# First stage of a two-block transformer kernel: separate columns for two weight chunks, earlier weight transfers, squares on GpSimd

## What is computed

```python
h = rmsnorm(x, a_norm1[i])                      # x: 1 x 512 x 1024
z = h @ a_w_in[i]                               # 1024 x (2 * 768 + 256)
u  = jax.nn.gelu(z[..., :TOK_WIDTH])            # TOK_WIDTH = 768
vv = jax.nn.gelu(z[..., TOK_WIDTH:2 * TOK_WIDTH])
q_mem = z[..., 2 * TOK_WIDTH:]
tok = gmlp_spatial_gating(u, vv, ...)
mem_o = memory_attention(q_mem, mem, a_mem_norm[i], a_w_mem_kv[i])
```

## Time and profile before

| what | value |
|---|---|
| median of 3 runs | 1449.86 us (1449.11 to 1451.22) |
| the profiled execution, its own time | 1451.27 us |
| its span, first to last instruction | 1449.5 us |
| TensorE matmuls, busy | 1438.8 us (99% of the span) |
| VectorE / ScalarE / GpSimd, busy | 961.8 / 669.5 / 41.0 us |
| granted TensorE clock, mean | 1.000 |

### The profile page before, as it was taken

One profiled execution on the slowest core, in us unless ns is written; L12 is line 12 of the kernel. 1 busy time (PEld: TensorE's weight loads), 2 busy tenths in 40 slices (PEclk: granted clock), 3 DMA queues, 4 the chain that ended last, 5 costly groups with the idle time before them and its releaser, 6 DMA issues.

```text
span 1449.5 us, 20006 instructions
## 1 busy us (share of the span) xinstructions
PE 1438.8 (99%) x7041; PEld 1151.6 (79%) x7041; DVE 961.8 (66%) x1579; ACT 669.5 (46%) x1100; POOL 41.0 (3%) x82
## 2 busy tenths in 40 slices
PE   8999999999999999999999999999999999999999
PEld 7978888888888887777778888888888877777777
DVE  5656777777766647555556777777677666666774
ACT  7445444444442235445454444444323356665662
POOL 0000000000001110000000000000111000000000
PEclk9999999999999999999999999999999999999999
DMA  6323222332346733212132322323677511112122
GB/s 227 124 96 117 73 90 98 101 97 91 101 138 236 235 112 119 76 59 88 61 100 73 101 90 98 101 90 115 203 241 234 163 56 59 59 58 74 59 82 94
DMA packets 44445, 162.66 MB, mean 112 GB/s; under 512 B 5076, under 2 KB 5844, under 8 KB 44384
## 3 DMA queue, kind: packets, MB, share of 16 engines
q1 hardware_dynamic: 33984, 126.44, 26.5%
q0 software_dynamic: 9104, 33.06, 6.7%
q10 hardware_dynamic: 1296, 2.36, 0.4%
HBM read 159.72 MB, written 2.12 MB: 112 GB/s over the span
## 4 chain that ended last, share of the span: by engine, by line
PE 93%; DVE 4%; DMA 2%; ACT 1%; issue 1%; POOL 0%; ACTq 0%; DVEq 0%; POOLq 0%
PE ps L383 17%; PE ps L384 17%; PE ps L385 17%; PE ps L399 5%; PE ps L401 5%; PE ps L400 5%; PE ps L1872 3%; PE ps L1874 3%; PE ps L1873 3%; PE ps L486 3%; PE ps L563 2%; PE ps L2050 1%; PE ps L551 1%; PE ps L1806 1%; PE ps L1808 1%; DVE wl L309 1%
## 5 line engine op out<-in xcount | busy, mean ns | idle before, releaser
L309 DVE TENSOR_TENSOR wl<-raw,wh 128x1024 fp32r<-128x1024 f32 (+3 forms) x199 | 253.9, 1276 | 119.0 <-ACT wh L303 118.8
L303 ACT CAST wh<-raw 128x1024 fp32r<-128x1024 f32 (+3 forms) x199 | 217.7, 1094 | 228.1 <-PE ps L385 194.8
L383 PE MATMUL ps<-xh,wh 128*128 128x512 f32 x720 | 281.1, 390 | 0.6 <-DVE hb L1416 0.6
L385 PE MATMUL ps<-xh,wl 128*128 128x512 f32 x720 | 280.2, 389 | 0.0
L384 PE MATMUL ps<-xl,wh 128*128 128x512 f32 x720 | 280.1, 389 | 0.0
L383 PEld LDWEIGHTS ps<-xh,wh 128*128 128x128 f32 x720 | 135.1, 188 | 30.0 <-issue 2.0
L384 PEld LDWEIGHTS ps<-xl,wh 128*128 128x128 f32 x720 | 135.1, 188 | 28.3 <-issue 0.5
L385 PEld LDWEIGHTS ps<-xh,wl 128*128 128x128 f32 x720 | 135.1, 188 | 28.2
L399 PE MATMUL ps<-xh,wh 128*128 128x512 f32 x344 | 144.5, 420 | 0.7 <-DVE wl L309 0.7
L383 PE MATMUL ps<-hth,wh 128*128 128x512 f32 x352 | 136.9, 389 | 0.0
L384 PE MATMUL ps<-htl,wh 128*128 128x512 f32 x352 | 136.9, 389 | 0.0
(11 more groups left out here) (310 smaller groups left out, 2337.3 us busy)
## 6 DMA issues: line engine op xcount, KB each, us to landing
raw<-w_a_f SPq DMA_DIRECT2D x44, 512.0 KB, 3.2
raw<-w_b_f SPq DMA_DIRECT2D x44, 512.0 KB, 3.2
row<-w_c_rows POOLq DMA_DIRECT2D x32, 512.0 KB, 4.6
row<-w_ada_rows POOLq DMA_DIRECT2D x24, 512.0 KB, 4.7
raw<-w_a_f SPq DMA_DIRECT2D x16, 704.0 KB, 4.1
raw<-w_b_f SPq DMA_DIRECT2D x16, 704.0 KB, 4.2
raw<-w_b_pair SPq DMA_DIRECT2D x18, 512.0 KB, 3.3
raw<-w_front SPq DMA_DIRECT2D x16, 512.0 KB, 3.3
```

Of the source, the lines that this page charges most:

```text
L303: nc.scalar.copy(wh[:, s, :width], raw[:, s, :width]).then_inc(w_hi, 1)
L309: nc.vector.tensor_tensor(wl[:, s, :width], raw[:, s, :width], wh[:, s, :width].bitcast(F32), ALU.subtract).then_inc(w_lo, 1)
L383: nc.tensor.matmul(dst, a, h(k), start=(k == 0), stop=False)
L385: mm = nc.tensor.matmul(dst, b, h(k), start=False, stop=(k == total - 1))
```

## The change

- Chunks 2 and 3 get columns of their own (`FRONT_COL`: from column 512 and from column 640 of their halves), beside chunks 0 and 1, which lie in the first 384 columns. So their loads no longer wait for the low parts of chunks 0 and 1, but only for the landing of chunks 0 and 1 (`w_raw` at 16), and their casts no longer wait for matmuls.
- SyncE's order: chunk 2 now ahead of x2 (rows 2, 3), the wait for x0 gone, chunk 3 ahead of x3, chunk 4 ahead of x4 (before, behind it), chunk 5 ahead of the two memory tiles.
- ScalarE squares only the row pairs 4, 5 and 6, 7. GpSimd squares the pairs 0, 1 and 2, 3 and adds the two.
- ScalarE and VectorE treat chunk 2 ahead of the rows 2 and 3.
- VectorE's first addition is gone and the second stands ahead of the low part of row 7.
- `mid()` stands inside block 7 of the first group, behind its first two token blocks (six matmuls); in the second group it stands where it was.

```diff
+FRONT_COL = {2: 512, 3: 640}
...
+        def front_at(n):
+
+            c = FRONT_COL.get(n, 0)
+            return slice(c, c + front_width(n))
...
                 kind, s = FRONT[n][0], n % 2
-                wait(sp, w_lo, n - 1)
+                if n in FRONT_COL:
+                    sp.wait_ge(w_raw[s], 16)
+                else:
+                    wait(sp, w_lo, n - 1)
...
             load_front(1)
-            sp.wait_ge(in_x[0], 16)
+            load_front(2)
             load_x(sp, 2)
-            load_front(2)
             load_front(3)
             load_x(sp, 3)
+            load_front(4)
             load_x(sp, 4)
-            load_front(4)
             sp.dma_start(kf[:, :2 * P], t["k_tiles"][:, :2 * P]).then_inc(in_id, 16)
+            load_front(5)
             for m in range(2):
                 sp.dma_start(memt[:, 4 * m:4 * m + 4, :], t["mem_t"][:, 4 * m:4 * m + 4, :]).then_inc(in_mem[m], 16)
-            load_front(5)
...
+            for e, m in enumerate((1, 2)):
+                pool.wait_ge(in_x[m], 16)
+                if e == 0:
+                    pool.wait_ge(in_x[0], 16)
+                x2 = xt[:, 2 * e:2 * e + 2, :]
+                nc.gpsimd.tensor_tensor(sqx[:, 2 * e:2 * e + 2, :], x2, x2, ALU.mult).then_inc(x_sqp, 1)
+            pool.wait_ge(x_sqp, 2)
+            nc.gpsimd.tensor_tensor(sqx[:, 0:2, :], sqx[:, 0:2, :], sqx[:, 2:4, :], ALU.add).then_inc(x_add, 1)
...
             def front_hi(n):
-                split_hi(act, n, n, front_width(n))
+                if n not in FRONT_COL:
+                    split_hi(act, n, n, front_width(n))
+                    return
+                act.wait_ge(w_raw[n % 2], 32)
+                nc.scalar.copy(wh[:, n % 2, front_at(n)], raw[:, n % 2, front_at(n)]).then_inc(w_hi, 1)
...
-            for k in (1, 2, 3):
-                first_hi(k)
+            first_hi(1)
             front_hi(2)
-            first_squares(0)
+            first_hi(2)
+            first_hi(3)
             front_hi(3)
             first_hi(4)
             first_hi(5)
-            first_squares(1)
+            first_squares(2)
             front_hi(4)
             first_hi(6)
             first_hi(7)
-            first_squares(2)
             act.wait_ge(x_add, 1)
             first_squares(3)
...
             def first_add(e):
-                dve.wait_ge(x_sq, e + 1)
-                wait(dve, x_add, e - 1)
+                dve.wait_ge(x_sq, e - 1)
+                dve.wait_ge(x_add, e - 1)
...
-                        if k == KD - 1:
-                            mid()
-                        c = (k - k0) * VW
+                        c = FRONT_COL.get(n, 0) + (k - k0) * VW
                         a, b = wh[:, s, c:c + VW], wl[:, s, c:c + VW]
                         for i in range(TT):
+                            if k == KD - 1 and i == (2, 0)[g]:
+                                mid()
```

More of the change, by code:

```diff
@@ L235, in build @@
         x_hi, x_lo = sem("x_hi"), sem("x_lo")
+        x_sqp = sem("x_sqp")
         x_sq, x_add = sem("x_sq"), sem("x_add")
@@ L758, in load_front @@
                     v = t["w_front"][i * P:(i + 1) * P, :]
-                sp.dma_start(raw[:, s, :front_width(n)], v).then_inc(w_raw[s], 16)
+                sp.dma_start(raw[:, s, front_at(n)], v).then_inc(w_raw[s], 16)
             load_front(0)
@@ L1220, in front_lo @@
             def front_lo(n):
-                split_lo(dve, n, n, front_width(n))
+                own = front_at(n)
+                dve.wait_ge(w_hi, n + 1)
+                nc.vector.tensor_tensor(wl[:, n % 2, own], raw[:, n % 2, own], wh[:, n % 2, own].bitcast(F32),
+                                        ALU.subtract).then_inc(w_lo, 1)
             def value_square(g, b):
@@ L1264, in _ @@
             front_lo(1)
-            for k in (1, 2, 3):
-                first_lo(k)
+            first_lo(1)
             front_lo(2)
+            first_lo(2)
+            first_lo(3)
             front_lo(3)
@@ L1270, in _ @@
             first_lo(5)
-            first_add(1)
             front_lo(4)
             first_lo(6)
+            first_add(2)
             first_lo(7)
-            first_add(2)
             first_add(3)
```

## The result

| | median | range | runs |
|---|---|---|---|
| before | 1449.98 us | 1448.86 to 1451.59 | 9 |
| changed | 1454.53 us | 1451.97 to 1455.27 | 9 |

The ratio is 1.0028, 95% interval 1.0018 to 1.0038: the change makes the kernel slower, by 4.5 us in the medians. The forecast was 1450.3 and the range ended at 1453.0. The profiled execution of the changed kernel took 1452.95 us (span 1451.1), one of its shorter ones; that of before took 1451.27, one of its longer ones. Two executions far outside the rest are left out of all that follows: one of 7507.45 us of the variant of experiment 2, and one of 2391.91 us (mean granted clock 0.556) of the kernel before beside the runs whose names start with d.

The account below looks back on a forecast made before the run. TensorE, busy 99% of the span, was taken as the bound, with 2.84 us of first-stage idle time to win. Terms of -0.3 and +0.7 gave +0.4 on 1451.27, so 1451.7, or 1450.3 for the median; range 1448.0 to 1453.0.

Parts of the forecast that it names:

- The first one also waits for the load of GpSimd's program: GpSimd's first square: program load, issued in the first microsecond, allows a start between about 5 and 8.9; 6.9 taken.
- the exclusion: VectorE's two-input operations and GpSimd's three were taken never to run at the same time; with short operations, chance 0.42.
- the 1.5 us wait at block 3: TensorE, first stage: block 3 starts at 14.0 behind chunk 3's low part, 1.5 us after block 2 ended.
- The price of an operation, 2.0 us,: Each of GpSimd's two squares and its addition on 1024 columns was taken to last 2.0 us.
- 1.8 and 3.3: Alternative lengths in us of a GpSimd operation, from two-input rows and from a one-input row of 128 columns.
- The 0.23 us seen on VectorE: Earlier trace: a VectorE low part beside a GpSimd operation took 1.85 us where the same form takes 1.62.
- Term one: First stage: the second group starts 0.3 us earlier than before, -0.3 us.
- Term two: Second group, block 6: 0.65 us wait for chunk 7 made by the sums' new place; +0.7 us with the semaphore.
- That execution is 1.4 us above the median: Profiled execution of before, 1451.27 against median 1449.86; so 1451.7 there became a median forecast of 1450.3.
- The granted clock is 1.00 throughout: Read from the profile windows of the kernel before; no term for a lowered clock in the sum.
- The slow rival: GpSimd becomes the bound at 3.3 us an operation: second group 2.7 us late, 1453.3 us; chance 0.14.
- the rival of late loads: First stage: reordered loads land 0.5 us later in a nearly full stream, without exclusion, 1449.5 us; chance 0.13.

Follow-up runs that it names:

- experiment 2: Changed kernel with the squares and additions of rows 0 to 3 back on ScalarE and VectorE: 1450.82 us beside 1449.60 for before.
- runs whose names start with d: Kernels timed on one chip: both of experiment 7, GpSimd memsets added to experiment 2's variant, and the repeated filler test; before beside experiment 7's kernels 1449.76 us.
- the two profiled executions of before: The kernel before, unaltered: first profile 1451.27 us; second, from the control run in the place of a tested kernel, 1450.02 us.
- experiment 6: Sums back ahead of block 7, in the changed kernel (1452.72 us) and in the variant of experiment 2 (1451.99 us), beside 1450.12 for before.
- Experiment 3: Kernel before with only GpSimd's two squares and addition in place of ScalarE's and VectorE's: 1453.13 us beside 1449.60 for before.
- the test with fillers: Changed kernel with twelve more warm-up matmuls on TensorE ahead of block 2, run twice: 1454.06 us and 1453.55 us.
- experiment 7: Variant of experiment 2 with VectorE's first addition ahead of chunk 4's low part (1450.21 us), then also chunk 7 ahead of memory-tile squares and additions (1449.16), beside 1449.76.

## Why the prediction was wrong

It said 1450.3, no change, and missed by more than its range.

- **"The first one also waits for the load of GpSimd's program ... I take the middle, 6.9."** This step failed first. The first square started at 5.22, the moment x1 had landed; the program's load held nothing up. The prediction's range took in a start at 5.0, but its sum never asked what the exclusion then does to row 0's low part, which ran from 5.22 in the kernel before. So the square met row 0's low part, on which block 0 waits, and the second square and the addition met chunk 2's and row 2's. Three hits ahead of block 2 instead of one; block 2 at 13.97 instead of 10.5, in place of the 1.5 us wait at block 3.
- **The price of an operation, 2.0 us,** was right (1.99 for the first, which started ahead of VectorE's; 2.25 and 2.55 where VectorE's had started first), and so was the exclusion, told from a single pair of rows. That the price was right is in part luck: 1.8 and 3.3 came from rows of 24 and 128 columns. (At 3.1 ns a column the second is 3.4, not 3.3.) The 0.23 us seen on VectorE in the earlier trace rows was the case in which VectorE's operation had started first; where GpSimd's had, VectorE lost 1.6 to 2.1 us.
- **Term one, -0.3 us,** was in truth +1.2 against the same profile (second group from 28.31 instead of 27.10, which the prediction put at 27.25) and 1.9 against an execution at the median.
- **Term two, +0.7 us,** was right in mechanism and place. The idle time was 0.67 us, as forecast, but the second group became 1.0 us longer by it (18.49 against 17.52 us).
- **"That execution is 1.4 us above the median"** was taken as an offset that carries over. More than half of it sat in the first stage itself (0.7 of the 1.25 us between the two profiled executions of before), so every wait of the new kernel was weighed against a stage that is 0.7 us shorter in an execution at the median.
- **"The granted clock is 1.00 throughout"** was said of before and silently kept for the changed kernel. This is the largest term that the sum lacked altogether: half of the runs lose another 1.8 to 2.0 us. No rival had it. The slow rival named GpSimd as the bound by long operations; the right one was GpSimd with operations of the length forecast, hitting earlier, and the clock behind that.
- **Loads:** chunk 2's cast started at 7.01 (forecast 7.3) and x2's rows at 8.35 (8.6). But chunk 4 was issued at 11.08, no earlier than before (10.76), because it waits for chunk 2's low part, which was among the delayed. Between 11 and 12 us the DMA engines stood nearly idle, as the share of 0.02 ahead of the 8 GB/s shows:

```profile
11.00:12.00 1.00, 0.36 (x3) 0.04 (x1) 1.00 (x2) 0.61 (x2) 1.00 (x1) 1.00 0.02 8
```

This looks like a loss and was none. Chunk 4 took 3.8 us to landing, so it was there at 14.9, and its cast started only at 16.40: it goes over the columns of chunk 2 and so waits for the last matmul of block 2, late by itself.

```profile
16.40 1.16 ACT L305 CAST wh<-raw 128x1152 fp32r<-128x1152 f32 x1 [2.34 <-PE ps L1778]
```

TensorE had blocks 2 to 4 to do meanwhile and did not wait for chunk 4 at all. Without GpSimd (the variant of experiment 2) chunk 4 was issued at 8.12 and had landed at 13.6, yet its cast started at 14.72, only 0.5 us before the 15.25 of the kernel before. There chunk 3 set the pace: issued at 5.7, 0.9 us earlier than before, it landed at 10.8, no earlier than before (10.7), and behind it ScalarE worked without a pause through its cast, a square, two high parts and another square. So the rival of late loads was right that the nearly full stream takes back what the new order gives, and ScalarE's squares take the rest.

The sum is now, against the runs of before on the same chip: 2.9 (stage) of the 3.2 us at 1.000, and 1.8 to 2.0 more in the runs with the lowered clock. The 0.3 us between 2.9 and 3.2 stay open. No profile of the changed kernel fell on a lowered clock; that it costs 1.7 us in one stretch is seen in the two profiles of experiment 6. That the wait before block 2 brings it is likely and not shown: the four kernels with unfilled waits of 1.3 us or more (the changed one, experiments 3 and 6) have a clock below 1.000 in 23 of 43 runs, before and the variants without such waits in 1 of 111, but the test with fillers is small.

## What to carry to other kernels

Work that is moved to GpSimd to relieve an engine is not free for VectorE: where GpSimd reads and VectorE's operations have two inputs, price it as VectorE's time, and look at which of VectorE's operations are next in line at the moment the data lands. In these kernels, waits of TensorE of 1.3 to 2.6 us went with a lowered clock that cost about as much again, in some executions only, so ask of every forecast whether it lengthens the longest wait, and look at the clock of each run and not only at that of the profiled one. Before a sum is made against one profiled execution, find out where its distance from the median lies.

## What the runs showed of the hardware that was not expected

- In the two profiles that show it, the clock fell to 0.50 for about 3.4 us, starting 0.8 and 1.8 us after TensorE had resumed work. By the mean clock it fell in 8 of 16 runs of the changed kernel, 5 of 10 and 7 of 11 of the two with the sums ahead, and in none of the 43 runs of before as tested kernel, of the variant of experiment 2 and of the two of experiment 7; of the 68 runs of before beside the experiments it fell in one. The first profile of before has a wait of 1.27 us and a clock of 1.000. With the wait filled it was below 1.000 in 1 of 13. Experiment 3 had 3 of 6, but two of those were as fast as the others (1452.91 and 1453.14 us).
- A memset on 1024 columns took GpSimd 0.95 us and a square that started ahead of VectorE's operation 1.99; the addition was always beside VectorE's work and took 2.55 us in the changed kernel.
- Of VectorE's two-input operations beside GpSimd's reading ones, those that had started second lost 1.6 to 2.1 us, those that had started first 0 to 0.2.
- The load of GpSimd's program cost nothing that can be seen.
